# Gated linear attention: each head's left side computed between the states and the outputs of the head in front

## The reference, cut to what matters

```python
b = jnp.cumsum(log_a, axis=3)                  # within a token chunk
q_t, k_t, k_end = q * jnp.exp(b), k * jnp.exp(-b), k * jnp.exp(b_last - b)
attn = jnp.where(mask, einsum("bhncd,bhnsd->bhncs", q_t, k_t), 0.0)
o_intra = einsum("bhncs,bhnse->bhnce", attn, v)
chunk_kv = einsum("bhncd,bhnce->bhnde", k_end, v)
# state n+1 = exp(b_last) * state n + chunk_kv n
o_inter = einsum("bhncd,bhnde->bhnce", q_t, s_in)
```

## Time and profile before

| | us |
|---|---|
| median of three runs | 1711.1 |
| lowest and highest of them | 1708.77, 1713.81 |
| the profiled execution | 1717.73 |
| its span, first to last instruction | 1716.4 |
| mean granted TensorE clock in it | 0.989 of full speed |

### The profile page before, as it was taken

How to read it: one execution, slowest core, us unless ns; L and a number is a source line. 1 busy time by engine, 2 the same in 40 slices (tenths; PEclk the granted TensorE clock), 3 DMA queues, 4 the chain that set the end, 5 groups by cost and what they waited for, 6 DMA issues and landing times. The chain is left out here.

```text
span 1716.4 us, 25051 instructions
## 1 busy us (share of the span) xinstructions
PE 1630.7 (95%) x10084; PEld 1421.3 (83%) x10084; DVE 1148.4 (67%) x1554; ACT 810.7 (47%) x1034; POOL 291.4 (17%) x239
## 2 busy tenths in 40 slices
PE   8999999899999989999999899989999999999997
PEld 7878888799987866899887598659798878889986
DVE  5777766488885656677467754478887655677764
ACT  5436554544333553444444243565544554356543
POOL 4743330000010010000005200037645000000000
PEclk9999999999999999999999899999999999999999
DMA  7544431377784530786454032000000165556553
GB/s 264 191 158 147 124 122 50 99 265 256 236 309 153 172 123 26 267 279 212 142 193 137 25 103 97 1 19 1 1 1 1 50 199 181 186 160 184 185 182 113
DMA packets 155394, 240.96 MB, mean 140 GB/s; under 512 B 12272, under 2 KB 80624, under 8 KB 155152
## 3 DMA queue, kind: packets, MB, share of 16 engines
q1 hardware_dynamic: 141632, 208.69, 37.2%
q0 software_dynamic: 6816, 27.08, 4.3%
q10 hardware_dynamic: 6832, 3.59, 0.8%
HBM read 238.29 MB, written 1.05 MB: 139 GB/s over the span
## 5 line engine op out<-in xcount | busy, mean ns | idle before, releaser
L196 DVE TENSOR_TENSOR wlo<-raw,whi 128x2048 fp32r<-128x2048 f32 x200 | 462.0, 2323 | 178.4 <-ACT whi L190 178.3
L190 ACT ACTIVATE whi<-raw 128x2048 fp32r<-128x2048 f32 x200 | 376.3, 1887 | 269.7 <-PE ps L330 177.3
L328 PE MATMUL ps<-xf,whi 128*128 128x256 f32 x1056 | 296.1, 280 | 2.9 <-DVE xf L476 1.0
L329 PE MATMUL ps<-xf,whi 128*128 128x256 f32 x1056 | 295.2, 280 | 0.0
L330 PE MATMUL ps<-xf,wlo 128*128 128x256 f32 x1056 | 295.2, 280 | 0.0
L328 PE MATMUL ps<-whi,xs 128*128 128x512 f32 x672 | 268.5, 400 | 9.2 <-DVE wlo L196 6.4
L330 PE MATMUL ps<-whi,xs 128*128 128x512 f32 x672 | 263.2, 392 | 0.0
L329 PE MATMUL ps<-wlo,xs 128*128 128x512 f32 x672 | 263.0, 391 | 0.0
L328 PEld LDWEIGHTS ps<-xf,whi 128*128 128x128 f32 x1056 | 198.4, 188 | 5.5 <-issue 5.4
L330 PEld LDWEIGHTS ps<-xf,wlo 128*128 128x128 f32 x1056 | 200.3, 190 | 0.0
L329 PEld LDWEIGHTS ps<-xf,whi 128*128 128x128 f32 x1056 | 199.2, 189 | 0.0
(11 more groups left out here) (369 smaller groups left out, 2638.4 us busy)
## 6 DMA issues: line engine op xcount, KB each, us to landing
raw<-in_ffn_w_gate_up SPq DMA_DIRECT2D x88, 512.0 KB, 5.0
raw<-in_a_w_in SPq DMA_DIRECT2D x72, 512.0 KB, 4.5
raw<-in_w_in SPq DMA_DIRECT2D x60, 512.0 KB, 4.6
wide<-in_w_mod POOLq DMA_DIRECT2D x24, 1024.0 KB, 6.8
raw<-in_w_up SPq DMA_DIRECT2D x44, 512.0 KB, 4.7
raw<-in_ffn_w_down SPq DMA_DIRECT2D x40, 512.0 KB, 4.6
raw<-in_b_w_in SPq DMA_DIRECT2D x24, 512.0 KB, 4.6
raw<-in_w_down SPq DMA_DIRECT2D x20, 512.0 KB, 4.1
```

Source lines behind the costliest of these rows:

```text
L190: self.hi_ok.inc(act.activation(self.whi[:, h % NHI, 0:nk, :], self.raw[:, h % NRAW, 0:nk, :], ACT.Copy))
L196: self.lo_ok.inc(dve.tensor_tensor(self.wlo[:, h % NRAW, 0:nk, :], self.raw[:, h % NRAW, 0:nk, :], self.whi[:, h % NHI, 0:nk, :].bitcast(F ...
L328: pe.matmul(o, ahi, bhi, start=start, stop=False)
L329: pe.matmul(o, ahi, blo, start=False, stop=False)
```

## The change

Layer b's heads are staggered.

- `left_pe`, `right_act`, `masked_dve`: a head's transposes and scores, their copy into `kt` and their masked copy into `AT_`. The left side of head h + 1 stands on TensorE between the state products and the outputs of head h. That of head 0 stands between the two halves of chunk 5.
- The state products come token chunk by token chunk for both directions, and raise `lb_kv` after the first two and after the third. `states_dve` does both directions in pairs. `result_dve(h - 1)` stands behind the states of head h; the low part of a result one head later still.
- `keep_warm` and `mid` go; the twelve first rows for bank 5 stand behind the last head.
- On ScalarE the high parts of chunk 5 stand in front of the wait for `e3` and behind the first exponential. The memsets stand at the head of VectorE's layer queue. There are three `qd` buffers and two `AT_`; state products use banks 4, 5 and 2, outputs of a head one bank, 6 or 7, and the result's transposes banks 3 and 0.

```diff
--- before.py
+++ after.py
@@ -1411,7 +1411,9 @@
         e1, e2 = la, c(2, GLA_HEADS * SEQ)
         e3 = t1
         dec = c(2, NB)
-        qd_, kd_, ke_ = ([c(2, SEQ) for _ in range(2)] for _ in range(3))
+        qd_, kd_, ke_ = ([c(2, SEQ) for _ in range(n)] for n in (3, 2, 2))
+        kt = [c(2, TT, P) for _ in range(2)]
+        AT_ = [c(TT, P) for _ in range(2)]
         at_ = Stage()
@@ -1432,10 +1434,14 @@
             pe.wait_ge(lb_evac.sem, 1)
             chunk_feat(chunks[1], range(0, 4))
             pe.wait_ge(lb_t1.sem, 1)
-            for j in range(4):
+            for j in range(3):
                 if j == 2:
                     pe.wait_ge(lb_evac.sem, 2)
                 chunk_tok(chunks[2 + j], ((4 + 2 * j) % 8, (5 + 2 * j) % 8))
+            chunk_tok(chunks[5], (2, 3), parts=(0,))
+            pe.wait_ge(lb_evac.sem, 5)
+            left_pe(0)
+            chunk_tok(chunks[5], (2, 3), parts=(1,))
@@ -1454,22 +1460,27 @@
             act.wait_ge(as_.sem, as_.n)
             lb_ln.inc(act.activation(t2, t2, ACT.Ln, bias=1.0))
             for j in range(4):
-                for h in later[2 + j]:
-                    W.hi(h)
+                if j != 2:
+                    for h in later[2 + j]:
+                        W.hi(h)
+                if j == 3:
+                    right_act(0)
                 W.wait_used(act, chunks[2 + j][1])
                 o_ = (v, r)[j // 2][:, :, (j % 2) * CW:(j % 2 + 1) * CW]
                 lb_evac.inc(act.activation(o_, ps[:, (4 + 2 * j) % 8:(4 + 2 * j) % 8 + 2, :], ACT.Copy if j < 2 else ACT.Silu))
                 if j == 1:
+                    W.hi(later[4][0])
                     act.wait_ge(lb_e3.sem, 1)
                     for d in range(2):
                         act.activation(dec[:, d, :], last[d], ACT.Exp)
                     act.activation(e1, t2, ACT.Exp)
+                    W.hi(later[4][1])
                     act.activation(e2, t2, ACT.Exp, scale=-1.0)
                     lb_ex.inc(act.activation(e3, e3, ACT.Exp))
 
         def scale_qk(h):
             hs = slice(h * SEQ, (h + 1) * SEQ)
-            qd, kd, ke = qd_[h % 2], kd_[h % 2], ke_[h % 2]
+            qd, kd, ke = qd_[h % 3], kd_[h % 2], ke_[h % 2]
@@ -1478,6 +1489,11 @@
 
         def project_dve():
             at_.meet(dve)
+            for a in AT_:
+                dve.memset(a, 0.0)
+            for q in range(2):
+                i_ = dve.memset(kt[q][64 - 64 * q:128 - 64 * q], 0.0)
+            lb_zero.inc(i_)
@@ -1516,8 +1532,49 @@
             dve.wait_ge(lb_ex.sem, 1)
             dve.wait_ge(lb_evac.sem, 2)
             scale_qk(0)
-            for h in later[5]:
-                W.lo(h)
+            W.lo(later[5][0])
+            scale_qk(1)
+            masked_dve(0)
+            W.lo(later[5][1])
+
+        mf, mb = const("gla_f").bitcast(I32), const("gla_b").bitcast(I32)
+
+        def left_pe(h):
+            qd, kd, ke = qd_[h % 3], kd_[h % 2], ke_[h % 2]
+            pe.wait_ge(lb_qk.sem, h + 1)
+            for d in range(2):
+                for t in range(TT):
+                    i_ = pe.transpose(ps[:, 0, (2 * d + t) * P:(2 * d + t + 1) * P], ke[:, d, t * P:(t + 1) * P], ident)
+            lb_ke.inc(i_)
+            if h:
...
+            lb_att.inc(i_)
...
+        def right_act(h):
+            act.wait_ge(lb_ke.sem, h + 1)
+            if h:
+                act.wait_ge(lb_kv.sem, 2 * h)
...
+            for q in range(2):
...
+            lb_kt.inc(i_)
+
+        def masked_dve(h):
+            if h >= 2:
+                dve.wait_ge(lb_o.sem, h - 1)
+            dve.wait_ge(lb_att.sem, h + 1)
+            for d, mk in ((0, mf), (1, mb)):
+                if d:
+                    dve.wait_ge(lb_at.sem, 2 * h + 1)
...
+                lb_at.inc(i_)
@@ -1526,64 +1583,49 @@
         c = Carve(-XS, 0)
         S = c(2, NCH, GLA_DV)
         sq, st = c(TT, GLA_DV), c(GLA_HEADS, TT)
-        kt = [c(2, TT, P) for _ in range(2)]
-        AT = c(TT, P)
-        mid = Stage()
-        mf, mb = const("gla_f").bitcast(I32), const("gla_b").bitcast(I32)
-        split, lo0 = Split(lambda t, k: r[:, t, k * P:(k + 1) * P], 1, None, banks=(5, 5, 0, 0)), xs_lo.n
+        split, lo0 = Split(lambda t, k: r[:, t, k * P:(k + 1) * P], 1, None, banks=(3, 3, 0, 0)), xs_lo.n
...
         def slot(d, j):
-            return ps[:, 2 + d, j * SEQ:(j + 1) * SEQ] if j < 2 else ps[:, 4, d * SEQ:(d + 1) * SEQ]
+            return ps[:, 4 + d, j * SEQ:(j + 1) * SEQ] if j < 2 else ps[:, 2, d * SEQ:(d + 1) * SEQ]
+
+        def o_at(h, t):
+            return ps[:, 6 + h % 2, t * GLA_DV:(t + 1) * GLA_DV]
 
         def heads_pe():
-            mid.meet(pe)
             for h in range(GLA_HEADS):
                 hv = slice(h * GLA_DV, (h + 1) * GLA_DV)
-                qd, kd, ke = qd_[h % 2], kd_[h % 2], ke_[h % 2]
-                pe.wait_ge(lb_qk.sem, h + 1)
...
-                lb_att.inc(i_)
+                qd = qd_[h % 3]
                 pe.wait_ge(lb_kt.sem, h + 1)
-                if h:
-                    pe.wait_ge(lb_s.sem, 2 * h)
-                for d in range(2):
-                    for j in range(NCH - 1):
-                        n = j if d == 0 else NCH - 1 - j
-                        i_ = pe.matmul(slot(d, j), kt[n % 2][:, d, n // 2, :], v[:, n // 2, hv], start=True, stop=True)
+                for js in ((0, 1), (2,)):
+                    if h == 0 and js == (2,):
+                        pe.wait_ge(lb_evac.sem, 6)
+                    for j in js:
+                        for d in range(2):
+                            n = j if d == 0 else NCH - 1 - j
+                            i_ = pe.matmul(slot(d, j), kt[n % 2][:, d, n // 2, :], v[:, n // 2, hv], start=True, stop=True)
                     lb_kv.inc(i_)
+                if h + 1 < GLA_HEADS:
+                    left_pe(h + 1)
+                pe.wait_ge(lb_at.sem, 2 * h + 2)
+                pe.wait_ge(lb_s.sem, h + 1)
+                if h >= 2:
+                    pe.wait_ge(lb_out.sem, 2 * (h - 1))
...
+                lb_o.inc(i_)
                 if h:
                     pe.wait_ge(lb_out.sem, 2 * h)
                     if h == 2:
                         pe.wait_ge(xs_lo.sem, lo0 + 1)
                     split.on_pe((h - 1,))
-                if h == GLA_HEADS - 1:
-                    first_rows(out_chunks[0], 5, 1, 1, range(HK))
-                else:
-                    keep_warm(6, 2)
-                pe.wait_ge(lb_at.sem, 2 * h + 2)
-                pe.wait_ge(lb_s.sem, 2 * h + 2)
...
-                    lb_o.inc(i_)
+            first_rows(out_chunks[0], 5, 1, 1, range(HK))
...
             prod_pe()
 
         def heads_act():
-            mid.meet(act)
             for h in range(GLA_HEADS):
-                act.wait_ge(lb_ke.sem, h + 1)
...
-                lb_kt.inc(i_)
+                if h + 1 < GLA_HEADS:
+                    right_act(h + 1)
+                act.wait_ge(lb_o.sem, h + 1)
+                for t in range(TT):
+                    as_.inc(act.activation(sq[:, t], o_at(h, t), ACT.Square, scale=GLA_DV ** -0.5, accum_out=st[:, h, t:t + 1]))
+                act.wait_ge(as_.sem, as_.n)
+                lb_rt.inc(act.activation(st[:, h], st[:, h], ACT.Sqrt, bias=eps_col))
                 if h:
                     split.on_act((h - 1,))
-                for t in range(TT):
...
-                lb_rt.inc(act.activation(st[:, h], st[:, h], ACT.Sqrt, bias=eps_col))
             split.on_act((GLA_HEADS - 1,))
...
+        def states_dve(h):
+            for j in range(NCH - 1):
+                if j != 1:
+                    dve.wait_ge(lb_kv.sem, 2 * h + (1 if j == 0 else 2))
+                if j:
+                    dve.wait_ge(vs.sem, vs.n)
+                for d in range(2):
+                    n = j if d == 0 else NCH - 1 - j
+                    to = n + 1 if d == 0 else n - 1
+                    if j == 0:
+                        i_ = dve.tensor_copy(S[:, d, to, :], slot(d, j))
+                    else:
+                        i_ = dve.scalar_tensor_tensor(S[:, d, to, :], S[:, d, n, :], dec[:, d, h * NCH + n:h * NCH + n + 1],
+                                                      slot(d, j), ALU.mult, ALU.add)
+                (lb_s if j == NCH - 2 else vs).inc(i_)
+
+        def result_dve(h):
...
+            dve.wait_ge(lb_rt.sem, h + 1)
...
+            dve.wait_ge(lb_gr.sem, 1 + h // 2)
...
         def heads_dve():
-            mid.meet(dve)
-            dve.memset(AT, 0.0)
...
             for h in range(GLA_HEADS):
-                hv = slice(h * GLA_DV, (h + 1) * GLA_DV)
+                states_dve(h)
                 if h:
-                    dve.wait_ge(lb_o.sem, 2 * h)
-                dve.wait_ge(lb_att.sem, h + 1)
...
-                for d in range(2):
-                    dve.wait_ge(lb_kv.sem, 2 * h + 2)
-                    for j in range(NCH - 1):
...
```

(69 more changed lines are left out.)

50 lines of the change are left out of this document (3 added, 47 removed).

## The result

Over nine runs of each, the changed kernel takes 1698.97 us in the median (1693.95 to 1703.55) and the kernel before 1712.46 (1707.35 to 1719.6). The medians lie 13.5 us apart. The ratio is 0.9911 (95% interval 0.9896 to 0.9927), which is 15.2 us, with 12.5 to 17.8 as its bounds. Six more runs of a later comparison gave 0.9917 (0.9897 to 0.9938). The forecast was -15.0 us, to 1696.1, with a range of 1690.5 to 1702.

The account below looks back on a forecast made before the run. No engine was full with useful work: each head was a chain from engine to engine. The stretch was to fall from 63.4 to 48.2 us, less 0.2 given back: -15.0, to 1696.1 us, range 1690.5 to 1702.

Parts of the forecast that it names:

- Chunk 5's halves: High halves earlier on ScalarE: TensorE's 2.55 us stall before chunk 5 and 1.71 of lower clock go; the exponentials' delay stays covered.
- the 1.71 of lower clock: Chunk 5 on TensorE: took 12.38 us instead of 10.67; the loss was to vanish with the stall in front.
- Head 0's left side: Transposes and scores in the middle of chunk 5: TensorE pays 1.55 us, inputs ready with about 2 us of slack.
- Heads: Each staggered head on TensorE: products to outputs 4.6 us, outputs 3.25, result transposes 0.49 three times; VectorE's other work hidden.
- products to outputs is 4.6: In each head, from state products to outputs: 4.6 us instead of 5.87, by VectorE's earlier release and states in pairs.
- The sum: Stretch from chunk 4's end to the output product's first rows: 48.2 us from 63.4, 0.2 given back, -15.0.
- The lower end of the range: 1690.5 us: states finishing under TensorE's 4.24 give 1.6 more, and runs spread by 2.5 about their median.
- The memsets: Four instead of three, moved to the start of VectorE's layer queue: cost nothing, without cover up to 4 us.
- GpSimd: Second product beside the first state copies: 0 taken, 1.6 us at most; the first meets a low half with slack.
- The step that failed: Heads on TensorE: `keep_warm` lay in the wait for the states, so removing it gives nothing by itself.
- the slower rival: Without `keep_warm` the clock is at 1.2 GHz for the whole head stage: +32 us, 1728; chance 0.04.
- the first rival: One clock fall (1.7 us) behind head 3's unfilled 1.9 us wait, or a port wait (1.6): 1697.8, both 1699.4; chance 0.28.

Follow-up runs that it names:

- e3: Not a run but a name in the code, without a measured time of its own: what ScalarE's exponentials make ready and `scale_qk(0)`, head 0's scaling on VectorE, reads.
- early_alone: Kernel before, with only chunk 5's high halves moved earlier on ScalarE; 0.9974 of the kernel before.
- no_warm: Kernel before without `keep_warm` in heads 0 to 2, nothing else; 1.0031 of the kernel before.
- late_halves: Changed kernel with chunk 5's high halves put back behind all exponentials; 0.9940 of the kernel before.
- pairs_alone: Kernel before with state products chunk by chunk and states in pairs, old order and `keep_warm` otherwise; 0.9992 of the kernel before.
- warm_again: Changed kernel with `keep_warm` put back in heads 0 to 2, between the next head's left side and the outputs; 0.9956 of the kernel before.
- result_first: Changed kernel with the result of the head in front ahead of the next states on VectorE; 0.9920 of the kernel before.
- by_direction: Changed kernel with state products and states one direction after the other, released once after all six products; 0.9950 of the kernel before.

## Why the prediction was right

**Chunk 5's halves.** The stall of 2.55 went and nothing was late next; `early_alone` gave 4.4 for 4.3. One reason in it was too firm: that the 1.71 of lower clock "follows that stall alone". With the same stall the clock fell in the kernel before and in `no_warm`, and not in `late_halves` and `pairs_alone`; all but `late_halves` have the same code up to there. So the term should be the cost of one fall times its chance, and that this part came out at the full 4.3 is luck in part: the profile that the forecast started from had a fall.

**Head 0's left side.** The slack was there as said. Chunk 5 with it took 12.25, where the sum had 10.9 + 1.55 and 0.2 for hand-overs, 12.65. The left side itself is 1.24 (619.61 to 620.85), not 1.55, because its last record overlaps the next step.

**Heads.** The step "products to outputs is 4.6" was 4.7: VectorE's release came after 1.93 to 2.03 (2.0 said), and the states took 2.64 (628.34 to 629.13 + 1.85), not 2.45, since a pair of state updates is 0.9 long rather than 0.8. That is inside my bounds of 2.45 and 2.82. Four heads make 18.9 instead of 18.4. The head's other terms, 3.25 and 0.49, were met. TensorE's own work stayed below it, and VectorE's queue was hidden as argued.

**The sum.** That it was met to 0.3 us in the stretch is luck in part: the heads came out 0.5 longer and chunk 5 with the left side 0.4 shorter, and these cancel. The lower end of the range was not what its terms give: 1696.1 less 1.6 less 2.5 is 1692.0, not 1690.5, and four times 4.6 - 4.24 is 1.4, not 1.6.

**The memsets.** Moved, they took 1.8 us of VectorE and no time of TensorE, as said.

**GpSimd.** I took 0 for its second product beside the states, by the masked copies, which lay beside it for only 0.7 of their 1.03 us. It was right. The first product now meets a low half that has time, also as said.

**The step that failed** is a side one: "`keep_warm` lay in the wait for the states, so its removal gives nothing by itself". In the old order its removal costs 4.5 us of lower clock, as `no_warm` shows. With the wait unfilled the clock fell in two of three heads. The removal cost nothing in the changed kernel, where the stagger puts the next head's left side in the same place and the waits of the first three heads are 0.6; `warm_again` shows that the filler has nothing left to earn there. So the slower rival had more behind it than its 0.04, had the stagger not filled the waits; the same holds for the first rival, since the clock did fall behind head 3's wait of 1.91 in two edits, though in neither profile of the changed kernel.

## What to carry to other kernels

When a loop's steps go from engine to engine, look for work of the next turn that depends on nothing in this one and put it where the engine waits; here that was worth a third to a half of the gain (5.2 to 7.7 of 15.3, by difference), and it also took over the filler's task of holding the clock. A filler is worth what the clock costs without it, so test it again each time the order changes: the same two matmuls earned 4.5 us and then cost 2.7. And release a chain after the part that it needs first: with the states in pairs that was 1.0 to 1.1 us in every staggered head, 0.9 of it from the earlier release and 0.2 from the pairs.

## What the runs showed of the hardware

The clock behind a wait isn't a fixed function of the wait. Waits of 2.54 to 2.57 in front of chunk 5 were followed by the lower clock in two profiles and not in two. In front of outputs, waits of 1.91 to 1.96 in head 3 were followed by it in two profiles (`late_halves`, `result_first`) and not in four, one of 2.19 and one of 3.01 were, one of 2.57 was and another in the same execution wasn't, and one of 2.96 (`by_direction`, head 3) wasn't. A fall cost 1.5 to 1.7 us each time but one, and 2.8 behind the wait of 3.01. What decides it is not shown.

The last feed-forward layer runs at one of two paces that the clock doesn't show. The same 90 us in two executions of the changed kernel, all of TensorE, granted clock 1.00 in both:

```profile
1530.00:1620.00 90.00, 90.00 (x766) 90.00 (x765) 70.96 (x96) 54.48 (x64) 0.00 (x0) 1.00 0.61 188
```

and in the repetition:

```profile
1530.00:1620.00 90.00, 90.00 (x796) 90.00 (x795) 72.64 (x100) 57.51 (x69) 0.00 (x0) 1.00 0.63 195
```

In the first execution 766 matmuls run in it, in the second 796: 0.1175 us against 0.1131 for each. The whole phase, from its first matmul to the first of the next phase, takes 124.45 us in the one (1507.80 to 1632.25) and 120.10 in the other (1507.72 to 1627.82), 4.35 us apart. Of twelve profiles six show the slow pace and six the fast; that of the kernel before and that of the changed kernel shown here are both slow, so this does not bias the comparison of their spans. Differences like this one help to explain why the runs of one kernel spread by some 10 us, which is wide beside an edit of 2 us. What sets the pace was not looked into.
